# Expert sums three tiles ahead of the query projection, row gathers in front of the store

## The reference, cut to what matters

```python
y = _hier_moe(tokens, ...)            # two experts of each row, weighted and summed
x = x + gt_f * y[:b * n].reshape(b, n, d)
if not last:
    xc = xc + gtc_f * y[b * n:].reshape(xc.shape)
# next layer:
h = _modulate(_rmsnorm(x, g_attn[i]), sh_a, sc_a)
hc = _modulate(_rmsnorm(xc, g_attn[i]), shc_a, scc_a)
q, k, v = _split_qkv(h, w_qkv[i])     # 1024 -> 1536 columns
# after the last layer: return _rmsnorm(x, g_final)
```

## Time and profile before

| | us |
|---|---|
| median of 3 runs | 3023.37 |
| lowest and highest run | 3021.78, 3028.12 |
| profiled execution, own time | 3018.33 |
| its span in the trace | 3016.6 |
| TensorE busy in it | 2783.2 (92%) |
| mean granted TensorE clock, share of full speed | 0.963 |
| experts of layer 0 end on TensorE, about | 1952 |
| first projection of layer 1 without an inner turn begins, about | 2032 |
| experts of layer 1 end on TensorE, about | 2956 |

### The profile page before, as it was taken

One profiled execution on the slowest core, in us unless ns is written; L12 is line 12 of the kernel. 1 busy time (PEld: TensorE's weight loads), 2 busy tenths in 40 slices (PEclk: granted clock), 3 DMA queues, 4 the chain that ended last, 5 costly groups with the idle time before them and its releaser, 6 DMA issues.

```text
span 3016.6 us, 65284 instructions
## 1 busy us (share of the span) xinstructions
PE 2783.2 (92%) x26993; PEld 1636.9 (54%) x26997; DVE 1133.1 (38%) x2743; ACT 749.6 (25%) x1575; POOL 330.3 (11%) x588
## 2 busy tenths in 40 slices
PE   7999999999889999998999999869999699999991
PEld 4444655444654456545666666534665466666660
DVE  2572653572654245453211221263443422112213
ACT  1111531111542156511111111142663111111111
POOL 2000530000530000011100010030000100100101
PEclk9999999999999999998999999989999799999996
DMA  7212653212643100048999999851001799999993
GB/s 240 84 56 84 226 158 96 83 56 84 230 163 127 56 29 2 16 163 316 401 401 397 404 402 399 334 190 43 2 2 43 300 389 404 399 396 403 403 367 108
DMA packets 155725, 637.70 MB, mean 211 GB/s; under 512 B 19776, under 2 KB 24384, under 8 KB 139184
## 3 DMA queue, kind: packets, MB, share of 16 engines
q1 hardware_dynamic: 114624, 517.59, 44.5%
q0 software_dynamic: 40944, 117.96, 11.6%
HBM read 583.48 MB, written 52.00 MB: 211 GB/s over the span
## 4 chain that ended last, share of the span: by engine, by line
PE 48%; DMA 2%; DVE 2%; issue 1%; ACT 1%; POOLq 0%; POOL 0%; DVEq 0%; ACTq 0%
PE SC L1199 15%; PE SC L1209 8%; PE PJ L1232 7%; PE PJ L1240 4%; PE PJ L1150 3%; PE TR L1185 2%; PE SC L1042 2%; PE PJ L1065 2%; PE TR L1055 2%; PE PJ L982 2%; PE TR L1219 1%; DMA XT<-h_rows,SMI 1%; DMA XS<-x_rows 1%; DVE PR L137 1%; DMA h_rows<-G 0%
## 5 line engine op out<-in xcount | busy, mean ns | idle before, releaser
L1002 PE MATMUL PJ<-WR,XT 128*128 128x512 f32 (+2 forms) x1152 | 474.1, 568 | 0.7 <-issue 0.7
L137 ACT ACTIVATE PT<-TR 128x512 f32<-128x512 f32 (+3 forms) x384 | 178.0, 494 | 904.9 <-PE TR L1219 735.2
L1002 PEld LDWEIGHTS PJ<-WR,XT 128*128 128x128 f32 x1152 | 216.1, 191 | 239.4 <-issue 214.3
L137 DVE TENSOR_TENSOR PR<-G 128x384 f32<-128x384 f32 x64 | 35.7, 558 | 737.5 <-ACT G L137 737.0
L982 PE MATMUL PJ<-WR,XT 128*128 128x512 f32 x576 | 256.6, 602 | 2.1 <-ACT XT L137 1.4
L137 DVE COPY XT<-PJ 32x256 f32<-32x256 f32 (+1 forms) x384 | 195.9, 510 | 143.9 <-PE PJ L1232 113.9
L1199 PE MATMUL SC<-WR,XT 128*64 128x256 f32 x2112 | 243.0, 383 | 0.0
L137 DVE TENSOR_REDUCE SM<-SC 128x1 f32<-128x768 f32 (+6 forms) x208 | 173.6, 835 | 169.4 <-PE SC L1042 162.5
L1150 PE MATMUL PJ<-WR,XT 128*128 128x512 f32 x512 | 227.2, 596 | 2.3 <-issue 2.3
L1199 PE MATMUL SC<-QK,XT 128*64 128x256 f32 x1984 | 226.2, 381 | 0.0
L1042 PE MATMUL SC<-QK 64*128 64x512 f32 (+7 forms) x512 | 188.6, 533 | 10.8 <-ACT PR L137 10.8
(11 more groups left out here) (208 smaller groups left out, 3143.2 us busy)
## 6 DMA issues: line engine op xcount, KB each, us to landing
WR<-in_w_gate_dram SPq DMA_DIRECT2D x34, 2048.0 KB, 9.1
QK<-in_w_down_dram SPq DMA_DIRECT2D x34, 2048.0 KB, 15.3
WR<-in_w_up_dram SPq DMA_DIRECT2D x32, 2048.0 KB, 13.8
QK<-in_w_up_dram SPq DMA_DIRECT2D x32, 2048.0 KB, 13.8
QK<-in_w_gate_dram SPq DMA_DIRECT2D x30, 2048.0 KB, 9.1
WR<-in_w_down_dram SPq DMA_DIRECT2D x30, 2048.0 KB, 15.5
WR<-in_w_ada_dram SPq DMA_DIRECT2D x24, 2048.0 KB, 8.0
WR<-in_w_in_dram SPq DMA_DIRECT2D x14, 2048.0 KB, 7.9
```

Of the source, the lines that this page charges most:

```text
L137: return lambda *a, **k: Signal(make(*a, **k), self)
L1002: m = mm(bank[:, 0:n], XT1[:, c, s.t * P:(s.t + 1) * P], w[:, c, 0:n], start=c == 0, stop=c == DC - 1)
```

## The change

Three things move, and no computation is added or removed.

In the plan, end 2 comes directly behind front 2, ahead of qkv(0). Inside the loop, front t+3 comes in front of qkv(t), and end t+3 behind it, for t = 0, 1, 2. So the order becomes front 2, end 2; front 3, qkv(0), end 3; front 4, qkv(1), end 4, qk_turn(0); front 5, qkv(2), end 5, qk_turn(1); qkv(3), qk_turn(2).

On POOL, the gathers and loads no longer stand in `combine`. The first combine issues the gathers of tiles 0 and 1 (their loads are issued during the experts, as before). `end(f)` now issues the gathers of tile f+2, the store of tile f, and the load of tile f+2, in that order. Both layers use this code, so the last layer's order on POOL changes too: before, gather 2, load 2, store 0, gather 3, load 3, store 1; now gather 2, store 0, load 2, gather 3, store 1, load 3.

```diff
@@ make_plan, the projection of layer 1
                 two = c < 2 and t < XT_TILES
+                far = 4 * c + t + 3
+                if l and far < len(combines):
+                    front(far)
                 ahead = combines[4 * c + t + 1] if l and 4 * c + t + 1 < len(combines) else None
...
                 prev.append(s)
-                if l and 4 * c + t + 2 < len(combines):
-                    add("combine_end", f=combines[4 * c + t + 2], l=l - 1)
-                    if 4 * c + t + 3 < len(combines):
-                        front(4 * c + t + 3)
+                if l and far < len(combines):
+                    add("combine_end", f=combines[far], l=l - 1)
                 flush2(1)
@@ make_plan, behind the experts of layer 0
             front(1)
             end(1)
             front(2)
+            end(2)
@@ POOL's program
                 if s.kind == "combine":
                     if s.t == 0:
                         gather_rows(s)
-                    nxt = by_fin.get(s.fin + 1)
-                    if nxt is not None and nxt.kind == "combine" and nxt.l == s.l:
-                        gather_rows(nxt)
-                        load_fin(nxt)
+                        gather_rows(by_fin[s.fin + 1])
                     last_fin = s
                 elif s.kind == "combine_end":
+                    after = by_fin.get(s.f.fin + 2)
+                    more = after is not None and after.kind == "combine" and after.l == s.f.l
+                    if more:
+                        gather_rows(after)
                     store_fin(s.f)
+                    if more:
+                        load_fin(after)
```

## The result

The changed kernel takes 3027.43 us (median of 18 runs, 3023.88 to 3029.9), the kernel before 3021.63 us over 18 runs: a ratio of 1.0019, interval [1.0012, 1.0025], or +5.8 us. The forecast was +3.7 us and 3027.1 us. The profiled execution has a span of 3027.2 us against 3016.6, but 3.9 of these 10.6 us lie ahead of anything that was changed: the first gather behind the experts of layer 0 starts at 1964.03 us instead of 1960.18. So all that follows is measured from that gather.

The account below looks back on a forecast made before the run. Neither PE nor DVE was taken as saturated: they wait for each other. Seam -0.5, clock +1.8 and end +2.4 summed to +3.7 us, on 3023.37 giving 3027.1 us; own range 3022 to 3031, with the rivals 3018.5 to 3034.

Parts of the forecast that it names:

- the four waits: PE idle before the inner turns of tiles 2 to 5, for DVE's scaled tile; 1.77 + 3 x 1.83 us.
- the seam: From the first gather behind layer 0's experts to the start of qkv(5); forecast -0.5 us without the clock.
- the end: Last layer, gather of tile 2 to last store: each load behind a store, 1.2 us later, twice: +2.4 us.
- The lead removes four waits: Before the turns of tiles 2 to 5: each tile finished a round earlier, so PE's waits go, -7.3 us.
- ACT in front of qkv(1): ACT squares tile 2 before copying turned tile 1 to XT: new PE wait of 3.5 us, between 3.1 and 6.0.
- ACT in front of the turn of tile 3: In qkv(2), ACT's QK copies stand behind end 4, which waits for tile 4's sums: PE waits 2.9 us.
- The clock: PE's clock falls to 1.2 GHz behind the new waits: first fall hidden, second costs +1.8 us.
- a sign of being wrong: In the last layer: the forecast is wrong if the last loads land as before, not 1.2 and 2.4 us later.
- Load 2 at the seam: Load of tile 2 before qkv(1): lands in near 3.4 us, gather 2 having landed, where it took 5.85 us.
- Rival 1: Between the layers: the four waits go, ACT's order does not bind; seam -7.3, end +2.4, thus 3018.5 us; chance 0.12.
- Rival 2: Between the layers: loads stay at 5.3 to 5.9 us, two clock falls; +12 in all, 3035.5 us; chance 0.19.
- the ring of store, load and sums: Store, load, sums and scaling close over two tiles: waits of 6 and 4.6 us, qkv(5) at about 2038, +6.3.

Follow-up runs that it names:

- e6: The changed kernel with the four stores to x_rows in the seam issued by SP on its own queue; ratio 1.0009 against the kernel before.
- e5: The changed kernel with PE kept busy by 28 transposes of the identity in each of its two long waits; ratio 1.0018 against the kernel before.
- e11: The changed kernel with PE kept busy by 28 transposes only in the wait before the turn of tile 3; ratio 1.0027 against the kernel before.
- e3: The changed kernel with the last layer's loads issued in front of its stores, as before; 3025.19 us, ratio 1.0013 against the kernel before.
- e1: The new order of steps with POOL's old program, in which end(f) issues only the store; ratio 1.0007 against the kernel before.
- e7: e1 with ACT's roots of tiles 2 and 3 behind the turned tile's copy, those of 4 and 5 behind the QK copies; ratio 1.0003 against the kernel before.
- e10: e7 with the roots of tiles 4 and 5 also behind the copy of the turned tile; 3016.61 us, ratio 0.9988 against the kernel before.
- e9: e8 with the roots of tiles 4 and 5 also behind the copy of the turned tile; 3017.49 us, ratio 0.9988 against the kernel before.
- e8: The changed kernel with e6's stores, e3's order at the end and the roots of tiles 2 and 3 late; ratio 0.9990 against the kernel before.

## Why the prediction was right

The time, the side and the mechanism held: the four waits go, and ACT's roots put two new ones in their place. The change is 0.19% (0.12 to 0.25), at the edge of the 0.2% that the forecast had as its limit. The sizes were off, and that 3027.43 us lies so near to 3027.1 is luck. The sum began at a median of 3023.37 us, which over 18 runs is 3021.63; the seam was put 4.4 us too low and the end 1.2 to 1.9 us too high.

- The lead removes four waits, -7.3 us: right. The rows show PE at 8.64 us between the last turns, and DVE kept up.
- ACT in front of qkv(1): forecast +3.5, measured 4.05 us, by the chain that was worked out. The load of tile 2 took 3.9 us where 3.4 was assumed, and DVE began 0.5 us after it had landed.
- ACT in front of the turn of tile 3: forecast +2.9, measured 4.22 us. The mis-sized term is the landing of a store behind a gather. Store 1 was to land near 1988.8, 5.7 us behind the 1983.11 of its issue before; it took 6.57 us, and store 2 took 7.34. By both together load 4 landed 44.8 us after the first gather, where the forecast's 2001.2 is 41.0. I had the stores behind the gathers in a queue; e6 shows that they are late on another queue too.
- The clock: one fall of 1.8 us with a hidden one before it was forecast. Both falls came, the second costs 2.9 us. That the first is hidden for the most part fits e5 and e11. But the forecast contradicts itself here. With its hidden fall PE comes to the second wait at 2007.0, and what is left up to 2008.1 is a wait of 1.1 us, less than the 1.8 us that left the clock at 1.00. By its own rows it had no second fall to count. The fall came because the stores were later than assumed and made the wait 4.22 us; where the wait was 1.30 us (e6) no fall came. So this term is right by luck.
- The seam is thus -7.3 + 4.05 + 4.22 + 1.9 + 2.9 = +5.8 against 5.7 measured. The first fall stands in this sum because the 4.22 us were counted after it had taken its share of the second wait. The forecast was +1.3 with the clock.
- The end: forecast +2.4, measured +0.5 between the two first traces and +1.2 over all. Here a sign of being wrong showed: the last two loads were to land 1.2 and 2.4 us later, and DVE took them up 0.2 us earlier and 0.5 us later, counted from the gather of tile 2 (0.3 and 1.2 us later in the means over all traces). The error is in the assumption that 512 KB of store delay the load by most of their own time. Load 2 took 4.3 us instead of the 5.62 of the earlier trace rows, load 3 4.68 instead of 4.52: a load behind a store pays little beyond its later issue. The ordered start of descriptors that the Trainium skill states ("DMA: Bandwidth & Descriptors", "Two DMAs through the same engine are not ordered") does not make the whole store's time fall on the load here; the same section says that they are pipelined, and the lower bound was nearer.
- Load 2 at the seam: the estimate of 3.2 us for 512 KB by the fit of the Trainium skill ("DMA: Bandwidth & Descriptors", "Anatomy of one DMA") is for a transfer alone, and so is the row of 3.4 us. Measured were 3.9 us, and 3.5 to 3.9 over the four loads, with a gather behind each. Both are nearer than the 5.85 us of the old place.

Rival 1 (all waits go) is refuted by both new waits. Rival 2 (loads stay at 5.3 to 5.9 us and the ring of store, load and sums closes) failed in the place it named: the loads were quick. But its ring did bind, through the stores, and its second wait of 4.6 us and its two falls that both count are nearer to what happened than the forecast's.

Seam and end of the two traces make 5.7 + 0.5 = 6.2 us, with the mean of the end 6.9; the measured ratio stands for +5.8 us, between 3.6 and 7.6. Open stays whether the clock falls behind both waits in every execution. Of the profiled executions with two such waits, the changed kernel and e3, both show both falls. Open is also by what resource two indirect gathers in flight make a store land 3 to 4 us later.

## What to carry to other kernels

Before a step is moved ahead, write down each engine's list anew and ask of every waiting instruction what now stands behind it: here the lead was good for PE and DVE, and a 1.6 us root on ScalarE, busy 25% of the span, ate it, because it waited for late data in front of copies that PE needed. Price a wait of the matrix engine of over about 2.5 us with a fall of its clock besides (here 2.55 us and more had one, single waits of 2.27 us and less had none), and measure the stretch, from one landmark to the next, where a change is near the noise of the whole. A store that a load waits for landed sooner when it was issued ahead of bulk gathers (2.9 to 4.0 us against 6.6 to 7.3), but in e1 the gathers then stood in front of the load, which took 5.1 to 6.0 us instead of 3.5 to 3.9. Store and load both ahead of the gathers was not run.

## What the runs showed of the hardware that was not expected

- A store of 512 KB landed in 2.9 to 4.0 us when it was issued in front of two gathers (e1). Behind them, in the changed kernel, the first took 3.8 us, issued 2.7 us after the second gather, and the others 6.6 to 7.3 us, issued directly behind it. A queue of its own (SP's) helped little: 4.6, 5.8, 7.1 and 5.6 us in e6.
- TensorE's clock fell to 1.2 GHz after every wait of 3.0 us and more in the seam (3.02 in e7 and e10, 3.57 in e9, 4.05 and 4.22 in the changed kernel), and stayed at 2.4 GHz through single waits of 1.8 us, and of 2.27 us in e8. But in e8 it fell behind two waits of 1.44 and 0.68 us that followed close on each other (eight matmuls in 5.29 us, granted clock 0.68 over 5.4 us), while it held behind 0.45 and 0.68 us in e5.
- The low clock did not last equally long: the first eight projection matmuls behind a fall took from 4.1 us (e7) to 6.7 us (e11) instead of 3.5, and e7 and e10 differ by 1.5 us behind the same wait.
